# A decoder layer on one core: x is transposed as it lands, and the roots of its RMSNorm are applied behind the input projection

## The reference, cut to what matters

```python
h = rms_norm(x, norm_mix_g)                  # x: 256 x 1024, y = x * rsqrt(mean(x*x) + 1e-6) * g
proj = h @ w_in                              # 1024 x 3080: fq fk fv (512 each), 8 forget logits, mq mk mv
fox  = forgetting_attention(fq, fk, fv, cumsum(log_sigmoid(f_logit + b_forget)))    # 8 heads of 64
moba = moba_attention(rotary(mq), rotary(mk), mv)      # 8 heads of 64; one block of 256, so causal softmax
x = x + concat(rms_norm(fox), rms_norm(moba)) @ w_out
h = rms_norm(x, norm_ffn_g)
x = x + moe(h)              # 32 experts of 3 x 1024 x 256 (gate, up, down), top 1 group of 4, top 2 in it
out = rms_norm(x, norm_final_g)
```

## Time and profile before

| | us |
|---|---|
| median of 3 runs | 363.54 |
| lowest, highest | 359.94, 366.21 |
| the profiled execution's time | 362.38 |
| its span, first to last instruction | 360.4 |
| PE busy | 311.8 (86%) |
| DVE, ACT, POOL busy | 163.1, 124.8, 42.6 |
| data moved by DMA | 121.19 MB |

### The profile page before, as it was taken

The page is one execution under the profiler, slowest core; times in us unless marked ns, Lnnn a source line. Parts: engine busy times, 40 slices in busy tenths (PEclk is TensorE's granted clock), DMA queues, the critical chain, the costliest instruction groups (busy, mean ns, idle before and its releaser), DMA issues.

```text
span 360.4 us, 11593 instructions
## 1 busy us (share of the span) xinstructions
PE 311.8 (86%) x4740; PEld 240.6 (67%) x4741; DVE 163.1 (45%) x451; ACT 124.8 (35%) x307; POOL 42.6 (12%) x74
## 2 busy tenths in 40 slices
PE   1799999999999989899979797989999989767381
PEld 1699989889875545776757575657676667645350
DVE  1645445383353612774445353435454445242234
ACT  4726336545241426532323132323332322221123
POOL 1200000363402225700000000000000000000002
PEclk9999999999999999999999999999999999899987
DMA  7999895062729999589999999999999999999923
GB/s 247 350 385 386 286 397 228 3 241 110 285 75 404 315 350 386 194 316 368 421 409 416 416 415 416 413 416 414 422 414 418 420 414 421 415 418 419 414 96 116
DMA packets 32652, 121.19 MB, mean 336 GB/s; under 512 B 5496, under 2 KB 7824, under 8 KB 24688
## 3 DMA queue, kind: packets, MB, share of 16 engines
q1 hardware_dynamic: 32480, 120.65, 85.5%
q10 hardware_dynamic: 144, 0.13, 0.1%
HBM read 119.72 MB, written 1.05 MB: 335 GB/s over the span
## 4 chain that ended last, share of the span: by engine, by line
PE 65%; DMA 14%; issue 6%; SPq 4%; DVE 3%; ACT 3%; DVEq 3%; POOLq 0%; POOL 0%; ACTq 0%
PE bank L494 13%; PE bank L739 8%; PE bank L561 7%; PE bank L488 7%; PE bank L772 7%; DMA ring<-in_w_up_dram 6%; DMA spare<-in_w_up_dram 6%; PE bank L699 6%; PE bank L706 4%; SPq L360 3%; PE bank L508 2%; PE bank L523 1%; PE bank L761 1%; PE bank L533 1%; DMA work<-in_x_dram 1%
## 5 line engine op out<-in xcount | busy, mean ns | idle before, releaser
L739 PE MATMUL bank<-ring,hT 128*32 128x128 f32 x1664 | 53.4, 279 | 14.9 <-issue 7.2
L739 PEld LDWEIGHTS bank<-ring,hT 128*32 128x32 f32 x1664 | 46.2, 112 | 26.4 <-issue 26.0
L1437 DVE SCALAR_TENSOR_TENSOR yb<-bank,pp,yb 64x512 fp32r<-64x512 f32 x36 | 27.0, 750 | 45.2 <-ACT yb L1019 44.6
L1183 DVE TENSOR_TENSOR unit_lo<-ring,unit_hi 128x2048 fp32r<-128x2048 f32 (+1 forms) x12 | 26.3, 2205 | 32.1 <-ACT unit_hi L841 32.0
L699 PE MATMUL bank<-pp,qk 128*128 128x64 bf16 x912 | 30.4, 194 | 5.7 <-DVE pp L1353 3.3
L699 PEld LDWEIGHTS bank<-pp,qk 128*128 128x128 bf16 x912 | 28.0, 98 | 10.7 <-DVE pp L1353 6.0
L1019 ACT ACTIVATE yb<-bank,pp 64x512 fp32r<-64x512 f32 x36 | 24.6, 682 | 28.9 <-PE bank L772 28.5
L561 PE MATMUL bank<-ring,qk 128*128 128x512 f32 (+1 forms) x72 | 29.9, 551 | 0.0
L1081 POOL TENSOR_TENSOR stats<-stats 128x1 f32<-128x1 f32 (+1 forms) x6 | 3.8, 634 | 218.7 <-DVE stats L1468 200.7
L739 PE MATMUL bank<-work,hT 128*32 128x128 f32 x320 | 20.9, 285 | 6.2 <-DMA spare<-in_w_gate_dram 3.0
L739 PEld LDWEIGHTS bank<-work,hT 128*32 128x32 f32 x320 | 18.2, 114 | 10.4 <-issue 10.3
(11 more groups left out here) (197 smaller groups left out, 510.2 us busy)
## 6 DMA issues: line engine op xcount, KB each, us to landing
ring<-in_w_up_dram SPq DMA_DIRECT2D x24, 1024.0 KB, 19.6
ring<-in_w_down_dram SPq DMA_DIRECT2D x24, 1024.0 KB, 19.5
ring<-in_w_gate_dram SPq DMA_DIRECT2D x22, 1024.0 KB, 18.8
ring<-in_w_in_dram SPq DMA_DIRECT2D x5, 2048.0 KB, 19.8
ring<-in_w_out_dram SPq DMA_DIRECT2D x4, 1024.0 KB, 8.7
spare<-in_w_gate_dram SPq DMA_DIRECT2D x4, 1024.0 KB, 19.4
spare<-in_w_up_dram SPq DMA_DIRECT2D x4, 1024.0 KB, 20.2
work<-in_w_gate_dram SPq DMA_DIRECT2D x4, 1024.0 KB, 17.8
```

Of the source, the lines that this page charges most:

```text
L739: last = mm(p_gu[b:b + CAP, w * P:(w + 1) * P], hg[:, k, CAP * e:CAP * (e + 1)], w_gu[at[e]][:, w, k, h, :], start=(k == 0), stop=(k == KD ...
L1183: V.tensor_tensor(unit_lo[b][:, k, :], unit_src(u)[:, k, :], unit_hi[b][:, k, :].bitcast(fp32), ALU.subtract).then_inc(w_lo_ready, 1)
L1437: V.scalar_tensor_tensor(out=yb[half][rest, :], in0=p_y[rows, :], scalar=wcol[rows, :], in1=yb[half][rows, :].bitcast(fp32), op0=ALU.mult, ...
```

## The change

- PE starts with 18 matmuls on a zeroed bf16 tile, whose result nobody reads.
- PE transposes the tiles of x as they land; the gains are transposed between the two tiles. `xn` is gone, and ACT's squares with it; DVE sums the squares (`xsq`).
- The roots (`rstdx`, POOL) are applied behind the projection. Where tokens are columns (fox q, k, forget logits), a row of the roots is wanted on all partitions: POOL scales the identity by them (`diag`), PE multiplies it by ones, DVE copies the result (`rootrow`) and multiplies q, k and logits by it as it takes them from PSUM. Where tokens are rows (units 4 to 11), ACT takes each bank in two pieces, each scaled by its tile's roots.
- The four gain vectors are issued from ACT's queue; `wf` goes behind unit 1; unit 0 comes in two transfers, each cast by itself, both behind all eight `h_hi`.
- Unit 0 runs as `first_unit()`: for each k both halves, into banks 0 and 2. Unit 2 waits until DVE has taken them.
- DVE takes the four q and k units in ACT's place; the counts of the waits on `act_took` shift by four.

The diff, cut to its core (declarations and shifted counts are left out):

```diff
-        xn = pp[:, 0:NT * D].rearrange("p (t d) -> p t d", t=NT)
+        xsq = pp[:, 0:NT * D].rearrange("p (t d) -> p t d", t=NT)
+        diag = pp[:, NT * D:NT * D + SEQ].rearrange("p (t c) -> p t c", t=NT)
+        rootrow = pp[:, NT * D + SEQ:NT * D + 2 * SEQ]
+        onesq = pp[:, NT * D + 2 * SEQ:NT * D + 2 * SEQ + P]
...
+        WARM = 18
+        first_bank = [bank[0], bank[2]]
         def wait_bank_free(pe, g):
+            if g == 2:
+                pe.wait_ge(qk_took, 1)
             if g >= 3:
-                if g - 3 < G_OF:
-                    pe.wait_ge(act_took, g - 2)
+                if g - 3 < G_FV:
+                    pe.wait_ge(qk_took, g - 2)
+                elif g - 3 < G_OF:
+                    pe.wait_ge(act_took, g - 2 - G_FV)
                 else:
                     pe.wait_ge(dve_took, g - 3 - G_OF + 1)
...
                 sp.dma_start(x[:, t, :], I["x"][0, t * P:(t + 1) * P, :]).then_inc(x_in[t], 16)
-            sp.dma_start(gvec[0:KD, :], I["norm_mix_g"][0].rearrange("(k p) -> k p", p=P)).then_inc(gv_in, 16)
-            sp.dma_start(gvec[KD:KD + 4, :], I["fox_out_g"][0].rearrange("(k p) -> k p", p=P)).then_inc(gv_in, 16)
-            sp.dma_start(gvec[KD + 4:2 * KD, :], I["moba_out_g"][0].rearrange("(k p) -> k p", p=P)).then_inc(gv_in, 16)
-            sp.dma_start(gvec[2 * KD:3 * KD, :], I["norm_ffn_g"][0].rearrange("(k p) -> k p", p=P)).then_inc(gv_in, 16)
-            sp.dma_start(wf, I["w_in"][0, :, 3 * FOX_W:3 * FOX_W + N_FOX].rearrange("(k p) c -> p k c", p=P)).then_inc(wf_in, 16)
...
                 c0 = b * FOX_W + (N_FOX if b >= 3 else 0)
                 if b == 0:
                     for u in range(2):
-                        sp.dma_start(unit_src(u), I["w_in"][0, :, u * UNIT:(u + 1) * UNIT].rearrange("(k p) c -> p k c", p=P)).then_inc(unit_in[u], 16)
+                        src = I["w_in"][0, :, u * UNIT:(u + 1) * UNIT].rearrange("(k p) c -> p k c", p=P)
+                        if u == 0:
+                            k = KD // 2
+                            sp.dma_start(unit_src(u)[:, 0:k], src[:, 0:k]).then_inc(first_in, 16)
+                            sp.dma_start(unit_src(u)[:, k:KD], src[:, k:KD]).then_inc(unit_in[u], 16)
+                        else:
+                            sp.dma_start(unit_src(u), src).then_inc(unit_in[u], 16)
+                    sp.dma_start(wf, I["w_in"][0, :, 3 * FOX_W:3 * FOX_W + N_FOX].rearrange("(k p) c -> p k c", p=P)).then_inc(wf_in, 16)
...
+            pe.wait_ge(zero_set, 1)
+            for i in range(WARM):
+                mm(bank[O_BANK][:, 0:SEQ], cpart[:, 0:P], cpart, start=True, stop=True)
             pe.wait_ge(cst_in, 16)
-            pe.wait_ge(gv_in, 64)
-            nc.tensor.transpose(bank[0][:, 0:3 * KD], gvec, ident[0:3 * KD, 0:3 * KD]).then_inc(gcol_t, 1)
             for t in range(NT):
-                pe.wait_ge(xn_ready, t + 1)
+                pe.wait_ge(x_in[t], 16)
                 for i in range(KD // 2):
                     for k in (2 * i, 2 * i + 1):
                         c = (k % 2) * SEQ + t * P
-                        last = nc.tensor.transpose(bank[4 + i][:, c:c + P], xn[:, t, k * P:(k + 1) * P], ident)
+                        last = nc.tensor.transpose(bank[4 + i][:, c:c + P], x[:, t, k * P:(k + 1) * P], ident)
                     if t == NT - 1:
                         last.then_inc(tr_done, 1)
+                if t == 0:
+                    pe.wait_ge(gv_in, 64)
+                    nc.tensor.transpose(bank[1][:, 0:3 * KD], gvec, ident[0:3 * KD, 0:3 * KD]).then_inc(gcol_t, 1)
+            pe.wait_ge(diag_ready, 1)
+            for t in range(NT):
+                last = mm(bank[O_BANK][:, t * P:(t + 1) * P], onesq, diag[:, t], start=True, stop=True)
+            last.then_inc(row_done, 1)
+            def first_unit():
+                hi, lo = unit_hi[0], unit_lo[0]
+                for n, (w, h) in enumerate(((hi, h_hi), (hi, h_lo), (lo, h_hi))):
+                    if n == 2:
+                        wait_split(pe, 0)
+                    for part in range(2):
+                        if n == 0:
+                            if part == 0:
+                                pe.wait_ge(half_hi_ready, 1)
+                            else:
+                                pe.wait_ge(w_hi_ready, 1)
+                        for k in range(part * KD // 2, (part + 1) * KD // 2):
+                            if n < 2:
+                                pe.wait_ge((h_hi_ready, h_lo_ready)[n], k + 1)
+                            for i in range(2):
+                                last = mm(first_bank[i][:, 0:SEQ], w[:, k, i * P:(i + 1) * P], h[:, k, :],
+                                          start=(n == 0 and k == 0), stop=(n == 2 and k == KD - 1))
+                last.then_inc(grp_done, 1)
...
+            first_unit()
             pe.wait_ge(gcol_set, 1)
-            unit(0)
             unit(1)
+            pe.wait_ge(row_ready, 1)
...
-            pe.wait_ge(act_took, G_FV)
+            pe.wait_ge(qk_took, G_FV)
             pe.wait_ge(fc_ready, 1)
...
             act.dma_start(cf[:, :], I["const_f32"]).then_inc(cst_in, 16)
-            for t in range(NT):
-                act.wait_ge(x_in[t], 16)
-                A(xn[:, t, :], x[:, t, :], ACT.Square, accum_out=ssq[:, t:t + 1]).then_inc(ssq_ready, 1)
+            act.dma_start(gvec[0:KD, :], I["norm_mix_g"][0].rearrange("(k p) -> k p", p=P)).then_inc(gv_in, 16)
+            act.dma_start(gvec[KD:KD + 4, :], I["fox_out_g"][0].rearrange("(k p) -> k p", p=P)).then_inc(gv_in, 16)
+            act.dma_start(gvec[KD + 4:2 * KD, :], I["moba_out_g"][0].rearrange("(k p) -> k p", p=P)).then_inc(gv_in, 16)
+            act.dma_start(gvec[2 * KD:3 * KD, :], I["norm_ffn_g"][0].rearrange("(k p) -> k p", p=P)).then_inc(gv_in, 16)
             act.wait_ge(gcol_t, 1)
-            nc.scalar.copy(gcol[:, :], bank[0][:, 0:3 * KD]).then_inc(gcol_set, 1)
+            nc.scalar.copy(gcol[:, :], bank[1][:, 0:3 * KD]).then_inc(gcol_set, 1)
             act.wait_ge(gcol_set, 1)
-            def took(g, dst, src):
+            def took(g, dst):
                 act.wait_ge(grp_done, g + 1)
-                nc.scalar.copy(dst, src).then_inc(act_took, 1)
+                for t in range(NT):
+                    last = A(dst[:, t], grp_bank(g)[:, t * UNIT:(t + 1) * UNIT], ACT.Copy, scale=rstdx[:, t:t + 1])
+                last.then_inc(act_took, 1)
...
             for k in range(KD):
-                if k == KD // 2:
-                    split_hi(0)
                 act.wait_ge(tr_done, k // 2 + 1)
                 A(h_hi[:, k, :], bank[4 + k // 2][:, (k % 2) * SEQ:(k % 2 + 1) * SEQ], ACT.Copy, scale=gcol[:, k:k + 1]).then_inc(h_hi_ready, 1)
+            k = slice(0, KD // 2)
+            act.wait_ge(first_in, 16)
+            nc.scalar.copy(unit_hi[0][:, k, :], unit_src(0)[:, k, :]).then_inc(half_hi_ready, 1)
+            k = slice(KD // 2, KD)
+            act.wait_ge(unit_in[0], 16)
+            nc.scalar.copy(unit_hi[0][:, k, :], unit_src(0)[:, k, :]).then_inc(w_hi_ready, 1)
             split_hi(1)
             act.wait_ge(wf_in, 16)
             nc.scalar.copy(wf_hi[:, :, :], wf).then_inc(wf_hi_ready, 1)
-            take_qk(0)
             split_hi(2)
-            take_qk(1)
             split_hi(3)
             split_hi(4)
-            act.wait_ge(fg_in, 48)
-            act.wait_ge(ft_done, 1)
-            A(fz, bank[O_BANK][0:N_FOX, 0:SEQ], ACT.Identity, bias=bfg).then_inc(fz_ready, 1)
             act.wait_ge(fa_ready, 1)
             step(A(fl, fa, ACT.Exp, scale=-1.0))
             A(fl, fl, ACT.Ln, bias=1.0).then_inc(fl_ready, 1)
-            take_qk(2)
             split_hi(5)
-            take_qk(3)
+            act.wait_ge(pow_ready, NT)
...
             step(nc.gpsimd.memset(mhalf, -0.5))
+            nc.gpsimd.memset(onesq, 1.0)
             for t in range(NT):
-                power(t, rstd, t, 1)
+                power(t, rstdx, t, 1)
+            pool.wait_ge(cst_in, 16)
+            for t in range(NT):
+                pool.wait_ge(pow_ready, t + 1)
+                last = nc.gpsimd.tensor_scalar(diag[:, t], ident, rstdx[:, t:t + 1], None, ALU.mult)
+            last.then_inc(diag_ready, 1)
             k = slice(0, KD // 2)
-            pool.wait_ge(w_hi_ready, 1)
+            pool.wait_ge(half_hi_ready, 1)
             nc.gpsimd.tensor_tensor(unit_lo[0][:, k, :], unit_src(0)[:, k, :], unit_hi[0][:, k, :].bitcast(fp32),
                                     ALU.subtract).then_inc(half_lo_ready, 1)
...
+            V.memset(cpart, 0.0).then_inc(zero_set, 1)
             for t in range(NT):
+                dve.wait_ge(x_in[t], 16)
+                V.scalar_tensor_tensor(out=xsq[:, t, :], in0=x[:, t, :], scalar=1.0, in1=x[:, t, :], op0=ALU.mult, op1=ALU.mult,
+                                       accum_out=ssq[:, t:t + 1]).then_inc(ssq_ready, 1)
                 dve.wait_ge(ssq_ready, t + 1)
```

(52 more changed lines are left out.)

5 lines of the change are left out of this document (2 added, 3 removed).

## The result

| | before | after |
|---|---|---|
| median (lowest to highest), 4 runs each, us | 361.9 (359.94 to 366.21) | 379.34 (377.06 to 380.62) |
| the profiled execution, its span, us | 362.38, 360.4 | 378.69, 376.9 |
| granted clock, mean over the span | 0.983 | 0.952 |

The runs of before are the three shown ahead and one more. The ratio is 1.0444, with an interval of 1.0381 to 1.0507: the change made the kernel 4.4% slower, where 361.2 us had been forecast. Executions over 1.5% above the fastest of their kernel (here the 366.21) are left out of every ratio and interval, but not of the medians. The loss is 16 to 17 us, and none of it is in the part that the diff edits.

The account below looks back on a forecast made before the run. From 158 us the stream of expert weights (181 us) was taken as the bound. A head 2.3 us earlier less 0.6 on ACT gave 1.7 less: 360.7 from the profiled execution, 361.8 from the median, taken as 361.2; range 357.5 to 364.6.

Parts of the forecast that it names:

- the last link of the path: From 147 us on: a microsecond won earlier starts the weight stream earlier and arrives whole, with the same 181 us behind.
- Rival 2: Couples' stage from 158 us: a slower stream or late couples give the gain back, 363.3 us; chance 0.17.
- the 1.7 us: Whole kernel: the net gain forecast, 2.3 us from the head less 0.6 us for ACT's two-piece takes.
- The head's start: PE's start: 18 warm-up matmuls from near 1.1 us, 4.1 us long, first transpose near 5.2, costing 0 to 0.1.
- The first tile's transposes: Head, behind the warm-up: eight transposes take 0.9 us, or 1.84 at the old speed, ending at 6.1 or 7.1.
- The gain vector: Head: the last one, issued by ACT at 2.1 to 2.4, lands at 6.8 (bounds 6.5 to 9.3); `h_hi` from 7.4.
- rival 3: Head: gain vectors land late on ACT's queue and hold up everything one for one, 364.4 us; chance 0.08.
- Unit 0: Head: starts at 11.5, first 16 matmuls at low clock, 7.52 us long, ends at 19.0, 2.3 us earlier.
- Rival 1: Unit 0: the clock stays high, so it takes 5.8 us and the gain is 3.4, 359.5 us; chance 0.2.
- ACT's pieces: Units 4 to 11, two pieces of 0.39 us: 0.3 more each, on the path at 70 and 94.5 us, cost 0.6.
- DVE's new work: Behind unit 0: four takes of 0.9 us and the logits, least slack 4.6 us, nothing on the path.
- The couples' stage: Expert part from 158 us: length unchanged, 181 us of stream; a changed length was listed as a sign of being wrong.

Follow-up runs that it names:

- e9: The changed kernel with 191 idle PE instructions and ACT casting unit 0's first half after four of eight `h_hi`: 360.4 us, ratio 0.9938.
- e7: The changed kernel plus 204 already-met waits on PE: 362.22 us, ratio 0.998 (0.994 to 1.002).
- e5: The kernel before plus 47 PE instructions that do nothing (already-met waits) ahead of the loop: 381.1 us, ratio 1.0506.
- e6: The kernel before plus 248 PE instructions that do nothing (already-met waits) ahead of the loop: 362.48 us, ratio 0.9992.
- e13: The kernel before plus 166 idle PE instructions ahead of the loop: 382.97 us, ratio 1.0539, two executions.
- e8: e7 with ACT casting the first half of unit 0 after four of the eight `h_hi`: 361.38 us, ratio 0.996.

## Why the prediction was wrong

- **The step that failed** is the last link of the path: behind the head the couples' stage was to follow "with the same 181 us behind", since "a microsecond won ahead of 147 us starts the stream a microsecond earlier and should arrive whole at the end". The change of that stage's length was put at nothing, without a reason; it was +17 us (183.2 to 200.2, first take to last). Nothing but microseconds was carried from the head to the couples. The diff hands the loop two things: a lead of 0.6 to 1.2 us and 47 PE instructions. I priced each new instruction by its duration (18 of 0.226 us, the row products 0.5), hid them behind other work, and never counted them. The page of before had a line for it, 22 transfers of instructions, and I read past it. No rival had it either: the slowest of them is 364.4, and the price was four times the widest gain that I considered (4.4).
- **The step by itself was right**, once the place is repaired: in e9 a lead of 3.2 us at unit 1 is 3.0 at the first take, 2.7 at the last and 2.7 in the medians. Rival 2, that no change arrives, has the interval of e9 against it, and its trace, in which 2.7 of the 3.0 us at the first take are still there at the last. For the kernel that was forecast, in a good place (e7), the runs can't tell the 1.7 us from none.
- **The head's start** was right to 0.1: warm-up from 1.07 to 5.09, first transpose at 5.05 (forecast 5.2).
- **The first tile's transposes** ran at the lower speed in spite of 4 us of products before them: 1.81 us for eight, the slow end of my two (0.9 or 1.84). The second eight took 1.09.
- **The gain vector** was issued at 2.43 and took 5.06 us to reach the chain's next link, forecast 4.67 from 2.1 to 2.4: PE had it at 7.53 and not 6.8 to 7.0, `h_hi` began at 8.24 and not 7.4. That is rival 3's mechanism, short of the 9.1 from which it would have turned the sign (PE had the gains at 7.53): 0.8 us of the gain lost.
- **Unit 0** took (20.10 - 12.26) = 7.8 us, forecast 7.52; low clock for the first sixteen as forecast (granted 0.50 from 10 to 16 us), and a little beyond (0.80 from 16 to 18), which is the 0.3. So unit 1 was 1.2 us early and not 2.3: both losses together are the missing microsecond. Rival 1, the high clock, didn't come in the kernel after. In e9, where unit 0 starts at 10.81 for 12.26, it did, but with a wait of 1.20 us for ACT the unit took 7.3 us and not 5.8. That its lead at unit 1 (3.2) is near rival 1's gain (3.4) is chance: 3.0 of it are the earlier start.
- **ACT's pieces** were priced at 0.6 us and cost 0.25 at most: the lead of 1.2 at unit 1 was 0.97 at 71 us and 0.95 at 94, so the second of the two places cost nothing. A piece took 0.47 to 0.52, not 0.39; at 69 us the two held the cast 0.36 longer than one copy did, and the cast itself was 0.12 shorter.
- **DVE's new work** kept PE waiting nowhere, as forecast; its takes lasted 0.41 to 0.43 a piece, and the first scores came 1.2 us early (46.01).
- **The couples' stage** had been the sign that I would be wrong: "if the couples' stage changes its length". I had listed the sign without asking what could move it.

## What to carry to other kernels

The loop of this kernel (1,731 instructions; smaller ones weren't tried) has a hidden input: its place in PE's program. 47 empty instructions ahead of it turned it from held to fetched, 22 transfers to 40 and +5.1% (e5), and 201 more turned it back (e6). So count instructions as well as microseconds, and compare the instruction lines of the DMA part (here 22 against 40) before reading anything else of a surprising result. If a change is to be judged by itself, bring both kernels to a good place with waits that are already met: here that turned +4.4% into -0.2% (e7, not clear of noise), and -0.6% with the head's order improved (e9).

## What the hardware showed that was not expected

- 248 waits that are already met cost PE nothing that can be measured (0.9992, 0.9953 to 1.003); 47 of them cost 5% by their place alone.
- At a return of the loop whose instructions were transferred again, PE stood for 6.4 to 8.2 us (ten runs; the shortest in e13, the longest in e8) while the DMA engines were full (share 1.00 to 1.07 from 263 to 269 us in the kernel after). A transfer of kind "instruction" on q8 is 16 KB (0.66 MB / 40).
- Transposes right behind 4.0 us of dense products were still slow (0.226 each), and the eight that followed a pause of 0.67 us and the gains' transpose were faster (0.14 each). e8 and e9 show the same, but in e7, whose head is that of the kernel after, the second eight were as slow as the first (1.97 us each eight), so it isn't the code alone. No run here explains it.
